# First loads in quarters, ScalarE's loads later, the first freed slot loaded in halves, and the bias rows of expert 0 behind its down product

## The reference

```python
proj = x @ w_in + b_in       # q, k, v, indexer q/k/weights, conv a/g, gate_attn, gate_conv
y_attn = dsa_attention(q, k, v, q_idx, k_idx, w_idx, rel_bias) @ w_o_attn   # 64 of the causal keys, T5 bias
y_conv = conformer_conv(conv_in, ...) @ w_o_conv                            # GLU, 31 taps, LayerNorm, swish
x1 = layer_norm(ALPHA * x + (sigmoid(g_attn) * y_attn + sigmoid(g_conv) * y_conv) @ w_out)
for e in range(32):          # MoE: every token goes to its 4 best experts
    gu = x1 @ w_gate_up[e] + b_gate_up[e]                # 1024 -> 2048
    g, u = min(gu[:, :1024], 7), clip(gu[:, 1024:], -7, 7)
    out += combine[:, e] * (((u + 1) * g * sigmoid(1.702 * g)) @ w_down[e] + b_down[e])
h = ALPHA * x1 + out
result = layer_norm(h + sigmoid(h @ w_ple_gate) * (p @ w_ple_proj))
```

## Time and profile before

| | before |
|---|---|
| median of 3 runs | 1190.86 us |
| profiled execution / its span | 1189.8 / 1188.0 us |
| TensorE busy | 1149.8 us, 97% |
| VectorE busy | 297.6 us, 25% |
| ScalarE busy | 172.5 us, 15% |
| moved by the DMA engines | 448.16 MB, mean 377 GB/s |
| DMA rate in the experts | 425 to 430 GB/s in most slices |

### The profile page before, as it was taken

The page is one execution under the profiler, slowest core; times in us unless marked ns, Lnnn a source line. Parts: engine busy times, 40 slices in busy tenths (PEclk is TensorE's granted clock), DMA queues, the critical chain, the costliest instruction groups (busy, mean ns, idle before and its releaser), DMA issues.

```text
span 1188.0 us, 13689 instructions
## 1 busy us (share of the span) xinstructions
PE 1149.8 (97%) x5606; PEld 578.4 (49%) x5606; DVE 297.6 (25%) x769; ACT 172.5 (15%) x335; POOL 11.5 (1%) x26
## 2 busy tenths in 40 slices
PE   7999999899999999999999899999999999999997
PEld 6888888734343434434344343434344343434346
DVE  0539932611111121211110211111212111111125
ACT  1204130111010111101110110101111011111112
POOL 0020000000000000000000000000000000000000
PEclk9999999999999999999998999999999999999999
DMA  9994466789999999999999999999999999999970
GB/s 325 346 297 142 142 251 245 268 339 428 427 427 428 428 427 427 426 428 428 428 425 426 426 400 429 427 429 426 428 429 425 430 424 430 425 428 426 430 335 36
DMA packets 64887, 448.16 MB, mean 377 GB/s; under 512 B 7120, under 2 KB 36080, under 8 KB 39984
## 3 DMA queue, kind: packets, MB, share of 16 engines
q1 hardware_dynamic: 58352, 440.84, 90.0%
q10 hardware_dynamic: 6464, 6.33, 1.6%
HBM read 444.53 MB, written 2.62 MB: 376 GB/s over the span
## 4 chain that ended last, share of the span: by engine, by line
PE 88%; DVE 4%; DMA 4%; ACT 1%; issue 1%; SPq 0%; DVEq 0%; ACTq 0%
PE bank L388 55%; PE bank L648 10%; PE bank L375 5%; DMA ring<-in_w_gu 3%; PE bank L408 3%; PE bank L777 2%; PE bank L790 2%; PE bank L1076 2%; PE bank L395 2%; PE bank L703 1%; DVE arena L434 1%; PE bank L382 1%; ACT arena L1244 1%; DVE arena L428 1%; DMA ring<-in_w_in 1%
## 5 line engine op out<-in xcount | busy, mean ns | idle before, releaser
L388 PE MATMUL bank<-ring,arena 128*64 128x512 f32 x1712 | 377.3, 594 | 6.5 <-DVE arena L434 4.1
L388 PE MATMUL bank<-arena 128*64 128x512 f32 x1456 | 322.8, 597 | 4.8 <-DVE arena L434 3.9
L388 PEld LDWEIGHTS bank<-ring,arena 128*64 128x64 f32 x1712 | 120.2, 137 | 241.6 <-issue 225.1
L388 PEld LDWEIGHTS bank<-arena 128*64 128x64 f32 x1456 | 101.9, 137 | 208.2 <-issue 193.6
L428 DVE TENSOR_TENSOR arena<-bank,arena 128x512 f32<-128x512 f32 x33 | 22.8, 692 | 612.7 <-PE bank L395 612.7
L648 PE MATMUL bank<-arena,ring 128*128 128x256 f32 x576 | 128.2, 383 | 0.2 <-DMA ring<-in_w_in 0.2
L648 PEld LDWEIGHTS bank<-arena,ring 128*128 128x128 f32 x576 | 109.8, 192 | 17.6 <-issue 2.8
L1244 ACT ACTIVATE arena<-bank 128x512 f32<-128x512 f32 x62 | 37.0, 597 | 397.1 <-PE bank L388 397.1
L375 PEld LDWEIGHTS bank<-sel,arena 128*128 128x128 f32 x512 | 63.0, 200 | 12.0 <-issue 11.4
L408 PE MATMUL bank<-arena 64*128 64x512 f32 x272 | 67.6, 615 | 1.3 <-ACT arena L1247 0.8
L375 PE MATMUL bank<-sel,arena 128*128 128x128 f32 x512 | 66.1, 289 | 0.5 <-DVE sel L461 0.5
(11 more groups left out here) (196 smaller groups left out, 529.1 us busy)
## 6 DMA issues: line engine op xcount, KB each, us to landing
ring<-in_w_gu SPq DMA_DIRECT2D x70, 2048.0 KB, 25.9
arena<-in_w_gu SPq DMA_DIRECT2D x58, 2048.0 KB, 27.4
ring<-in_w_dn SPq DMA_DIRECT2D x35, 2048.0 KB, 25.7
arena<-in_w_dn SPq DMA_DIRECT2D x29, 2048.0 KB, 26.6
ring<-in_w_in SPq DMA_DIRECT2D x19, 1024.0 KB, 12.9
ring<-in_w_out SPq DMA_DIRECT2D x4, 1024.0 KB, 5.4
arena<-in_w_pg SPq DMA_DIRECT2D x2, 2048.0 KB, 44.7
ring<-in_w_oa SPq DMA_DIRECT2D x2, 1024.0 KB, 6.1
```

The lines of the kernel that those rows point to most:

```text
L388: mm = pe.matmul(to[half * CAP:(half + 1) * CAP, :], rows, w[:, half * 512:(half + 1) * 512], start=first, stop=last)
```

## The change

- The first chunk and `xT` are loaded in quarters of two blocks of rows. TensorE works on both tiles of chunk 0 at once, block by block, and multiplies the bias table after them.
- ScalarE issues six loads at first. The write of the bias table comes after the fourth `evac`; behind it stand six of the other loads; the last three (`bgu`, `x`, `pT`) stand behind the copies that the indexer waits for.
- Load 11 is issued as two halves: the first when TensorE has done the first block of rows of expert 0 (`half_used`), the second when it has done two, as before.
- In expert 0, `turn_bias` and the adding of the bias rows stand behind down. ScalarE's copy stands behind its sigmoid.

```diff
+            turn_of[i] += 2 if n == ES else 1
 def load_pair(sp, n, e, c):
+    if n == ES:
+        for half in range(2):
+            at = slice(half * SLOT, (half + 1) * SLOT)
+            sp.wait_ge(*((chunk_used, 1) if half else (half_used, 1)))
+            sp.dma_start(slot_of(n)[:, at], pair_source(e, c)[:, at]).then_inc(e_in[slot_no[n]], 16)
+        return
...
-for half in range(2):
-    ks = slice(half * HK, (half + 1) * HK)
+for quarter in range(4):
+    ks = slice(2 * quarter, 2 * quarter + 2)
...
+for k in range(KD):
+    if k % 2 == 0:
+        pe.wait_ge(xT_in[k // 2], 16)
+        pe.wait_ge(first_in[k // 2], 16)
+    for j in range(2):
+        mm = pe.matmul(bank[tiles.n + j][:, 0:S], w_view(0)[:, k, j * P:(j + 1) * P], xT_sb[:, k, :],
+                       start=(k == 0), stop=(k == KD - 1))
+        if k == KD - 1:
+            mm.then_inc(tile_done, 1)
+tiles.up(2)
 pe.wait_ge(relb_in, 32)
 pe.wait_ge(relb_copied, 1)
 pe.matmul(bank[7][:, 0:S + P], relb_copies, oneh_sb[:, :], start=True, stop=True).then_inc(tab_done, 1)
-two(0)
 two(1)
...
 read_flag(pe, flag, e + 1)
-if e == 0:
-    turn_bias(gate_sum)
-before(e)
+if e:
+    before(e)
...
-use_down(e, weights)
+use_down(e, weights, 3 if e else 2)
+if e == 0:
+    turn_bias(gate_sum)
+    before(e).then_inc(d_done, 1)
...
 sums_out(e)
-if e == 0:
-    bias_out(gate_sum)
 read_flag(a, flag, e + 1)
 sigmoid(a, e, 0, False)
 next_gathered(e)
 embedded(e)
+if e == 0:
+    bias_out(gate_sum)
 a.wait_ge(d_done, 3 * e + 3)
```

More of the change, by code:

```diff
@@ L512, in _ @@
             def _(sp):
-                HK, (what, c0, n) = KD // 2, FRONT[0]
-                for half in range(2):
-                    ks = slice(half * HK, (half + 1) * HK)
-                    rows = slice(half * HK * P, (half + 1) * HK * P)
-                    sp.dma_start(xT_sb[:, ks, :], xT[rows, :].rearrange("(k p) t -> p k t", p=P)).then_inc(xT_in[half], 16)
+                what, c0, n = FRONT[0]
+                for quarter in range(4):
+                    ks = slice(2 * quarter, 2 * quarter + 2)
+                    rows = slice(2 * quarter * P, (2 * quarter + 2) * P)
+                    sp.dma_start(xT_sb[:, ks, :], xT[rows, :].rearrange("(k p) t -> p k t", p=P)
+                                 ).then_inc(xT_in[quarter], 16)
                     sp.dma_start(w_view(0)[:, ks, :], src[what][rows, c0:c0 + n].rearrange("(k p) c -> p k c", p=P)
-                                 ).then_inc(first_in[half], 16)
+                                 ).then_inc(first_in[quarter], 16)
                 for i, (what, c0, n) in enumerate(FRONT):
@@ L876, in use_gate_up @@
                         mm = part(k, 1, w[:, at])
+                        if wait_xt and k == 0:
+                            mm.then_inc(half_used, 1)
                         if k % 2 == 1:
@@ L894, in use_gate_up_twice, with use_down @@
                                 mm.then_inc(gu_done, 1)
+                        if e == 0 and k == 0:
+                            mm.then_inc(half_used, 1)
                         if k in (1, 3, 5):
                             mm.then_inc(chunk_used, 1)
-                def use_down(e, weights):
+                def use_down(e, weights, done=3):
                     pe.wait_ge(t_read, e * 2 + 2)
@@ L908, in use_down @@
                             mm.then_inc(chunk_used, 1)
[L909 removed]
+                    mm.then_inc(d_done, done)
                 def use_down_twice(e, weights):
@@ L933, in rows_of @@
                     pe.wait_ge(rows_out, e * 2 + 2)
-                    combine(pe, q, last=last, done=done)
+                    return combine(pe, q, last=last, done=done)
                 def next_gather(e):
@@ L943, in before @@
                         pe.wait_ge(bias_ready, 1)
-                        combine(pe, 1, first=True)
-                    else:
-                        rows_of(e - 1, 1 - e % 2)
+                        return combine(pe, 1, first=True)
+                    return rows_of(e - 1, 1 - e % 2)
                 def turn_bias(to):
@@ L1143, in evac @@
                     cnt.up()
+                for j in range(2):
+                    evac(qiT[:, j, :], ACT.Identity, bT_sb[:, j:j + 1])
                 a.wait_ge(tab_done, 1)
                 a.activation(tab_sb, bank[7][:, 0:S + P], ACT.Identity).then_inc(tab_ready, 1)
-                for j in range(2):
+                for j in range(2, 4):
                     evac(qiT[:, j, :], ACT.Identity, bT_sb[:, j:j + 1])
```

36 lines of the change are left out of this document (15 added, 21 removed).

## The result

| | before | changed |
|---|---|---|
| median | 1190.55 us (6 runs, 1188.95 to 1192.21) | 1200.2 us (6 runs, 1197.52 to 1205.9) |
| ratio | | 1.0087, 95% interval 1.0070 to 1.0104 |
| profiled execution / span | 1189.8 / 1188.0 us | 1204.68 / 1202.9 us |
| TensorE busy | 1149.8 us, 97% | 1160.1 us, 96% |

The forecast was 1192.4 us with a range to 1195.0; the kernel takes 9.65 us more than before, not 1.5. The profiled execution of the changed kernel is one of its longer ones. So a second profile of the same kernel was taken (span 1196.6 us, in the last set of experiments), and both are used.

A forecast was written before the change was run, and what follows sets the result against it. TensorE, not the weight stream, was taken to set the end. A front gain of 1.3 us and an expert 0 loss of 2.8 us gave +1.5 us on the median 1190.86, so 1192.4 us, range 1189.3 to 1195.0.

The forecast's parts named there:

- What bounds the kernel: Whole run: TensorE, busy 97%, sets the end; moving it ahead of 700 us moves the end by as much.
- Step 4: Front, ScalarE's loads behind the table's write: no effect, copies over at 30.0 us, wanted at 32.7, 2.7 us to spare.
- Rival C: Front: ScalarE hangs in its queue behind the table's write, TensorE waits 1.75 us; +3.25 us, 1194.1 us; chance 0.18.
- Step 2: Expert 0, bias rows behind down: products lie bare for 2.94 us, down begins 0.12 us earlier; net 2.8 us later.
- Step 1: Front, quarters and both tiles at once: chunk 1 begins at 15.3 us, 1.3 us earlier; ends 13.9 to 16.9.
- No quarter is late: Front: the second, third and fourth quarters land before TensorE wants them at about 8.5, 11 and 13.5 us.
- Step 3: Load 11 in halves, expert 0: the stream's 1.8 us lead is eaten by the hole at 686 to 710 us; nothing gained.
- The holes at 690 to 712 us: DMA stream behind the long expert: its holes near 690 to 712 us grow by 3 to 5 us in all.

The follow-up runs named there:

- wr_last: The changed kernel with the router's weights issued as ScalarE's last load, behind `pT`; ratio 1.0022 to the kernel before.
- write_last: The changed kernel with ScalarE's six late loads issued ahead of the table's write instead of behind it; ratio 1.0038 to the kernel before.
- b_fill: The kernel before with expert 0's bias rows behind down and idle products put where they were, ahead of down; 1193.63 us, ratio 1.0027.
- b_only: The kernel before with only the bias rows of expert 0 moved behind its down; ratio 1.0045.
- q_only: The kernel before with only the quarters and TensorE's work on both tiles at once; ratio 1.0008.
- best: The kernel before with the quarters and ScalarE's loads and write moved, but the router's weights loaded at the start; 1189.56 us, ratio 0.9990.
- l_first: The kernel before with ScalarE's loads and write moved, router's weights at the start, no quarters, old order at the front; 1191.19 us, ratio 0.9998.
- h_only: The kernel before with only load 11 issued in two halves; ratio 1.0006.

## Why the prediction was wrong

**What bounds the kernel: right for this change, and not in general.** What moved TensorE ahead of 700 us moved the end: in the first profile the shift was 14.1 us at expert 1, 15.6 behind the long expert (which lost 1.5 us more, in part at a low clock) and 14.9 at the end; in the second 9.3, 9.3 and 8.6. The weight waits at the end fell from 1.0 to 0.6 and 0.5 us. But in two profiles TensorE left the long expert earlier than before, by 1.9 us (`wr_last`) and 1.4 us (`write_last`), and the end came 0.4 and 2.1 us later than before all the same. There the stream had no hole worth the name (418 to 428 GB/s in windows of 10 us from 680 to 720 us in `wr_last`, before down to 385), and TensorE waited 2.6 and 2.8 us for weights in the last experts. From `wr_last`:

```profile
PE bank L395 <- DMA ring<-in_w_gu: 2.1, 2, 1.2
PE bank L395 <- DMA arena<-in_w_gu: 0.5, 1, 0.5
```

So "whatever moves TensorE ahead of 700 us moves the end by as much" holds only as long as there is a hole to give up. Before, the mean rate over 680 to 720 us was 407 of 427 GB/s, so the holes held 1.9 us of the stream in all.

**Step 4, "ScalarE's loads later: nothing": wrong, and the first of the two steps that failed.** The term was 5.2 us of issue time with 2.7 us to spare. It was 11.8 us, and TensorE waited for the last 2.5 of them. I carried durations from one place in the program to another. There the six loads had stood behind six small ones; here they stand behind a write of 1.5 MB. Even the row that warned me was misread: L1130's 2.28 us I took for a property of that load. It is the load behind the router's weights, and there it took 0.96 to 2.28 us without the write ahead and 6.64 to 6.75 with it; with the write and without these weights ahead it took 0.94 to 1.53. Rival C named the mechanism, but I priced a hold by SyncE's 3.66 us and its consequence by the wait alone, 1.75 us; it was 6.75 us of hold, 3.15 of wait, and 3.1 more of low clock behind it. A chance of 0.18 was too little for a rival that needed only 2.7 us.

**Step 2, "bias rows behind down: the loss": its sum was exact and not complete, the second failure.** Forecast +2.8 us; `b_fill` has 2.8. Down's start moved forward by 0.15 us against the turn of expert 0 in `b_only` and by 0.08 in `b_fill`; I had taken 0.12. What I left out is that the work taken away was also what kept TensorE from standing still for 3.35 us. The prediction had both ends of the hole in hand, since it used both to place down, and it had used a low clock for the front. It never asked whether this new hole would bring it back. That made +5.2 us of +2.8. I had even written bounds of 2.7 to 2.9: a width that holds only as long as nothing but the moved pieces changes.

**Step 1, "quarters: the gain": right in direction, too large in size.** Chunk 1 was forecast at 15.3 us, ends 13.9 to 16.9; the five profiles have 15.8 in the mean, a gain of 0.8 us where 1.3 was forecast, and one of them 17.57, outside the ends. Work began at 4.7 to 4.8 us, forecast 5.0; from there to the table's product it took 9.2 to 11.95 us, 10.2 in the mean, forecast 9.6; the table's product and the step to chunk 1 took 0.84 us, forecast 0.66. The 1.2 GHz in this term was read from the spacing of the records alone: the granted clock is printed as 1.00 in every window from 0 to 18 us, in the kernel before and in the changed one. "No quarter is late" was wrong in three of the five, by 0.2 to 0.7 us. With ScalarE's loads at the start the gain is gone: `q_only`, 16.43 us. So steps 1 and 4 were not separate: the quarters' gain showed only with ScalarE's loads out of the way. The rule of the Trainium skill against loads under 1 MiB ("DMA: Bandwidth & Descriptors", rules for kernel authors) did not decide here: `best` against `l_first` is quarters against halves, and the quarters are not behind (0.9990 and 0.9998, with intervals that overlap). By the estimate from the Trainium skill (same page, anatomy of one DMA) 256 KB take 2.6 us; that section gives it for loads that GpSimd issues, and these are SyncE's. Here the fastest quarter of `xT` took 2.9 us from issue to landing and the fastest of the weights 3.4, so the trace differs from it.

**Step 3, "halves: nothing": right in its number, not in its mechanism.** 1.0006 (0.9998 to 1.0015), and the waits for weights at the end are unchanged. But in the one profile of `h_only` the lead of the stream did not go into the hole at 686 to 710 us; it was gone by 300 us for the most part.

**The holes at 690 to 712 us** were to grow by 3 to 5 us. Over 40 us of windows, 694 to 734 us here against 680 to 720 before, the mean rate fell from 407 to 381 GB/s, 1.0 MB or 2.4 us of the stream; in the second profile (690 to 730 us) it was 395, 1.1 us. The direction is right, the size less.

## What to carry to other kernels

An issue's duration belongs to what stands ahead of it in its queue, not to the load alone: the same 16 KB took 0.94 to 6.75 us to issue, the most behind a write of 1.5 MB and a load of a thousand short rows, and its engine stood still for as long. So before work that the busiest engine waits for is put behind such loads, measure their issues in that place. Before work is moved out of a place where TensorE would otherwise wait, look at how long the hole becomes: the granted clock of the windows behind comparable holes says what it costs, and here that was 2.4 us beside 2.8 for the work itself.

## What the runs showed that I had not expected

- Behind a hole of 3.35 us ahead of down the granted clock was 0.50 (1.2 GHz) in all six profiles that had it unfilled (down 8.42 to 10.08 us); with 0.73 us, behind other short work, down took 7.09 us.
- A load of 16 KB took 6.64 to 6.75 us to issue behind the write and the router's weights, and 1.06 us (`wr_last`) without the latter. Behind the write alone single issues still took up to 2.07 us.
- The hold can move on without harm: the two reads of the bias table took 9.92 us to issue in `wr_last` and 5.94 in `best` (1.04 us before), with no wait of TensorE for them there. The write had landed by then in both, and in `best` the router's weights stood at the start. So this hold has another cause, which is open.
- Identical instructions began chunk 1 at 14.78 to 17.57 us. So single profiles of this front differ by up to 2.8 us, as much as the largest of the terms I added up.
- Where the long expert kept its clock (granted 1.00 from 620 to 640 us in `wr_last`, 0.74 before) TensorE ran into the stream of weights: it was 1.9 us ahead of the kernel before at 681 us and 0.4 us behind it at the end, and 1.6 us of that is more waiting for weights.
